# The second block's crossings by token tile, with the norm's gain and shift applied to rows

## The reference

```
for layer in range(DEPTH):                       # second block, DEPTH = 2
    mod = einsum('bd,dn->bn', silu(c), w_ada[layer]) + b_ada[layer]
    sh1, sc1, gt1, sh2, sc2, gt2 = split(mod, 6)
    h = rms_norm(x, g_attn[layer]) * (1.0 + sc1) + sh1
    y = hybrid_mixer(h, ..., w_in[layer], w_out[layer], ...)
    x = x + gt1 * y
    h = rms_norm(x, g_ffn[layer]) * (1.0 + sc2) + sh2
    f = swiglu(h, ...) if layer == 0 else moe_swiglu(h, ...)   # 8 experts, 2 per token
    x = x + gt2 * f
```

## Time and profile before

| | |
|---|---|
| median of 3 runs | 1899.09 us (1898.74 to 1899.36) |
| the profiled execution: its time, its span | 1900.42 us, 1898.6 us |
| PE busy | 1805.7 us, 95% |
| DVE busy | 1424.7 us, 75% |
| ACT busy | 1114.9 us, 59% |
| POOL busy | 392.4 us, 21% |
| the chain that ended last | PE 83%, DVE 6%, issue 6%, ACT 4%, POOL 1% |
| mean granted clock of PE | 0.983 |

### The profile page before, as it was taken

The page is one execution under the profiler, slowest core; times in us unless marked ns, Lnnn a source line. Parts: engine busy times, 40 slices in busy tenths (PEclk is TensorE's granted clock), DMA queues, the critical chain, the costliest instruction groups (busy, mean ns, idle before and its releaser), DMA issues.

```text
span 1898.6 us, 25852 instructions
## 1 busy us (share of the span) xinstructions
PE 1805.7 (95%) x8703; PEld 1469.8 (77%) x8703; DVE 1424.7 (75%) x1667; ACT 1114.9 (59%) x1296; POOL 392.4 (21%) x315
## 2 busy tenths in 40 slices
PE   7899999989999997899989779999999999999997
PEld 6678886858888785788878568888888888888885
DVE  5758874476876585654457659888888888889897
ACT  6745444565443454444355537777777777777775
POOL 3722213463212362200046400000000000000000
PEclk9999999999999999899999989999999999999999
DMA  8348994418897341465544249999999999999994
GB/s 272 112 176 331 338 350 136 154 46 333 335 355 277 90 156 45 158 197 180 191 156 155 98 169 361 384 381 380 380 380 383 378 381 384 381 380 379 382 380 169
DMA packets 237933, 506.37 MB, mean 267 GB/s; under 512 B 23304, under 2 KB 74720, under 8 KB 231712
## 3 DMA queue, kind: packets, MB, share of 16 engines
q1 hardware_dynamic: 225664, 492.85, 71.4%
q0 software_dynamic: 3008, 10.32, 2.0%
q10 hardware_dynamic: 9184, 2.23, 0.5%
HBM read 497.42 MB, written 7.91 MB: 266 GB/s over the span
## 4 chain that ended last, share of the span: by engine, by line
PE 83%; issue 6%; DVE 6%; ACT 4%; POOL 1%; DMA 0%; POOLq 0%; SPq 0%; DVEq 0%; ACTq 0%
PE bank L2391 26%; PE bank L2393 25%; PE bank L2392 25%; PE bank L2510 2%; ACT slab L2080 1%; ACT w_hi L1930 1%; PE bank L2836 1%; DVE slab L1317 1%; PE bank L2602 1%; PE bank L2579 1%; POOL w_lo L848 1%; PE bank L2547 0%; DVE x L1096 0%; PE bank L2561 0%; DMA slab<-in_w_in 0%
## 5 line engine op out<-in xcount | busy, mean ns | idle before, releaser
L999 DVE TENSOR_TENSOR w_lo<-slab,w_hi 128x2048 fp32r<-128x2048 f32 x369 | 848.0, 2309 | 211.6 <-ACT w_hi L1930 211.0
L1930 ACT ACTIVATE w_hi<-slab 128x2048 fp32r<-128x2048 f32 (+2 forms) x421 | 796.7, 1899 | 330.1 <-PE bank L2393 245.7
L2391 PE MATMUL bank<-w_hi,hT_hi 128*128 128x512 f32 (+3 forms) x1664 | 648.5, 390 | 15.1 <-DVE hT_lo L1048 4.3
L2393 PE MATMUL bank<-w_hi,hT_lo 128*128 128x512 f32 (+3 forms) x1664 | 637.3, 383 | 0.0
L2392 PE MATMUL bank<-w_lo,hT_hi 128*128 128x512 f32 (+3 forms) x1664 | 636.8, 383 | 0.0
L2391 PEld LDWEIGHTS bank<-w_hi,hT_hi 128*128 128x128 f32 x1664 | 315.3, 189 | 77.8 <-DVE w_lo L999 8.8
L2393 PEld LDWEIGHTS bank<-w_hi,hT_lo 128*128 128x128 f32 x1664 | 314.7, 189 | 59.4
L2392 PEld LDWEIGHTS bank<-w_lo,hT_hi 128*128 128x128 f32 x1664 | 315.5, 190 | 55.1
L848 POOL TENSOR_TENSOR w_lo<-slab,w_hi 128x512 fp32r<-128x512 f32 (+2 forms) x208 | 256.0, 1266 | 376.6 <-ACT w_hi L1930 359.7
L2391 PE MATMUL bank<-w_hi,hid_hi 128*128 128x512 f32 x680 | 265.7, 391 | 0.7 <-DVE w_lo L999 0.7
L2393 PE MATMUL bank<-w_hi,hid_lo 128*128 128x512 f32 x680 | 265.0, 390 | 0.0
(11 more groups left out here) (254 smaller groups left out, 1229.6 us busy)
## 6 DMA issues: line engine op xcount, KB each, us to landing
slab<-in_w_exp_gate SPq DMA_DIRECT2D x176, 512.0 KB, 7.0
slab<-in_w_exp_up SPq DMA_DIRECT2D x176, 512.0 KB, 7.4
slab<-in_w_exp_down SPq DMA_DIRECT2D x176, 512.0 KB, 6.8
slab<-in_w_ada SPq DMA_DIRECT2D x48, 1024.0 KB, 5.9
slab<-in_w_mlp_in SPq DMA_DIRECT2D x64, 512.0 KB, 6.3
slab<-in_w_mlp_out SPq DMA_DIRECT2D x64, 512.0 KB, 9.0
slab<-in_w_in SPq DMA_DIRECT2D x56, 512.0 KB, 5.1
slab<-in_w_out SPq DMA_DIRECT2D x32, 512.0 KB, 4.7
```

What stands on the lines that cost most here:

```text
L999: dve.tensor_tensor(w_lo[:, q, 0:n], raw(s)[:, 0:n], w_hi[:, q, 0:n].bitcast(F32), ALU.subtract).then_inc(lo_dve, 1)
L1930: act.activation(w_hi[:, q, 0:n], raw(s)[:, 0:n], ACT.Copy).then_inc(hi_done, 1)
L2391: pe.matmul(dst, a_hi, b_hi, start=start, stop=False)
L2393: return pe.matmul(dst, a_lo, b_hi, start=False, stop=stop_)
```

## The change

In the second block each crossing works by token tile. The gain and the shift come as rows that every partition holds: `mod_gains` makes the gain columns early (in the MLP of the layer before), ACT stores them to DRAM with elements of 4 bytes, SP loads gain and shift back, broadcast to 128 partitions (two loads of 512 KB per crossing, `gain_loads`). DVE multiplies each quarter of x by the gain row (`gained_part`, or a whole row in crossing 1) and then scales by the root and adds the shift row in one instruction (`scaled_row`). PE turns the 8 chunks of one token tile, four to a PSUM bank; ACT and DVE write `hT_hi` and `hT_lo` of four chunks at once straight from PSUM. PE finishes the sum of token tile 0 before that of tile 1, and the next products of token tile 0 before those of tile 1. Besides: the output projection's tile 1 moves in front of the last `values()`; the split slots of the MLP's and the experts' tiles start at 3, those of l = 3 at 2; both roots stand behind POOL's weight pieces; the third weight tile of l = 2 and 3 goes from POOL to DVE; the weights of l = 3's first tiles are rounded by ACT before its last `hid_high_part`; and the transposes back to rows in crossing 4 are gone.

```diff
-        BY_DVE1, BY_DVE2 = range(2, 6), range(3, 5)
+        BY_DVE1, BY_DVE2 = range(2, 6), range(2, 5)
...
+            def gain_loads(l, which):
+                m = l - DEPTH
+                sp.wait_ge(gains_out, 32 * (m + 1))
+                if m:
+                    sp.wait_ge(xn_done, TT * (which + 1))
+                for to, src in zip(gain_rows(which), (gains[m, which:which + 1, :].broadcast_to([P, D]), mod_row(m, 3 * which))):
+                    sp.dma_start(to, src).then_inc(gains_in, 16)
...
                     gated(wg, wu, 0)
+                    sp.wait_ge(av_done, UNIT0[l] + UNITS[l])
+                    gain_loads(l, 1)
                     pool_lo(FF0[l] + 1)
...
-                        ff_lo(l, 0, norm_roots)
+                        ff_lo(l, 0)
                         ff_lo(l, 1)
-                    else:
-                        norm_roots()
+                    norm_roots()
...
+            def scaled_row(t, which, root):
+                dve.wait_ge(rstd_done, root)
+                dve.scalar_tensor_tensor(h[:, t, :], h[:, t, :], stat[:, 2, t:t + 1], gain_rows(which)[1], ALU.mult, ALU.add
+                                         ).then_inc(xn_done, 1)
+            def turn(t, b, l, which):
+                o = slice(t * P, (t + 1) * P)
+                dve.wait_ge(hh_done, splits_before(turn_at(l, which)) + 2 * t + b + 1)
+                dve.tensor_tensor(hT_lo[:, 4 * b:4 * b + 4, o], turned_half(l, which, t, b), hT_hi[:, 4 * b:4 * b + 4, o].bitcast(F32),
+                                  ALU.subtract).then_inc(hl_done, 1)
...
+            def cross_gated(l, which):                      # on ACT
+                square_part(0, 0)
+                square_part(1, 0)
+                square_part(0, 1)
+                turn(0, 0, l, which)
+                turn(0, 1, l, which)
+                if not which:
+                    hi_of(l, 2)
+                square_part(1, 1)
+                turn(1, 0, l, which)
+                turn(1, 1, l, which)
...
+            def down_by_token(at):                          # on PE, l = 2's last MLP step
...
+                        part(0, 0, before_last, False)
+                        part(0, 1, before_last, False)
+                        turn_step(J - 1)
+                        part(1, 0, before_last, False)
+                        pe.wait_ge(hidl_done, at + 2 * TT)
+                        last = next_low()
+                        part(0, 0, last, True).then_inc(part_done, 1)
+                        part(0, 1, last, True).then_inc(part_done, 1)
+                        part(1, 1, before_last, False).then_inc(w_used, 1)
+                        part(1, 0, last, True).then_inc(part_done, 1)
+                        part(1, 1, last, True).then_inc(w_used, 1)
+                        turn_row(0, l + 1, 0)
```

More of the change, by code:

```diff
@@ L91 @@
 X_SELW = 7424
-X_HTF = 6144
+X_HTF, X_GAIN = 6144, 2048
 X_ADA, X_ACT, X_ACT2 = 0, 6144, 7168
@@ L160, in stage, with slot @@
     def stage(self, raw=RAW, split=SPLIT, base=0):
[L161 removed]
+        self.last = {self.slot(self.i - 1 - k): self.t - 1 - k for k in range(min(self.split, self.i - self.at))}
         self.i, self.raw, self.split, self.base, self.start, self.at = 0, raw, split, base, self.t, 0
+    def slot(self, i):
+        return (self.base + i % self.split) % SPLIT
     def mark(self):
@@ L1025, in _ @@
-            sums, roots, turned, xns, updates, parted = [0], [0], [0], [0], [0], [0]
-            def turn(gain, shift, banks):
-                m = turned[0]
-                turned[0] += 1
-                def low_of(k):
-                    dve.wait_ge(hh_done, splits_before(m) + k + 1)
-                    dve.tensor_tensor(hT_lo[:, k, :], htf[:, k, :], hT_hi[:, k, :].bitcast(F32), ALU.subtract).then_inc(hl_done, 1)
-                for k in range(KC):
-                    dve.wait_ge(tp_done, KC * m + k - k % 2 + 2)
-                    src = bank[banks[k // 2]][:, (k % 2) * SEQ:(k % 2 + 1) * SEQ]
-                    dve.tensor_scalar(htf[:, k, :], src, gain(k), shift(k), ALU.mult, ALU.add).then_inc(tpe_done, 1)
-                    if k:
-                        low_of(k - 1)
-                low_of(KC - 1)
+                    gained_row(t, 0)
@@ new lines, in norm, with gained_row, gains_loaded @@
+                for t in range(TT):
+                    scaled_row(t, 0, roots[0] - TT + t + 1)
+            sums, roots, turned, gained, updates, parted = [0], [0], [0], [0], [0], [0]
+            def gained_row(t, which):
+                link(dve.tensor_tensor(h[:, t, :], x[:, t, :], gain_rows(which)[0], ALU.mult))
+            def gains_loaded():
+                gained[0] += 1
+                dve.wait_ge(gains_in, 32 * gained[0])
+            def scaled_row(t, which, root):
+                dve.wait_ge(rstd_done, root)
+                dve.scalar_tensor_tensor(h[:, t, :], h[:, t, :], stat[:, 2, t:t + 1], gain_rows(which)[1], ALU.mult, ALU.add
+                                         ).then_inc(xn_done, 1)
@@ L2008, in ada_columns, with gain_stores @@
                         act.dma_start(to.unsqueeze(2), mod_columns(l, v).unsqueeze(2)).then_inc(mods_in[l], 16)
+            def gain_stores(m):
+                act.wait_ge(gains_made, 2 * m + 2)
+                with nc.allow_non_contiguous_dma(reason="columns to rows"):
+                    for which in range(2):
+                        act.dma_start(gains[m, which].rearrange("(k p) -> p k", p=P).unsqueeze(2), modg[:, m, which, :].unsqueeze(2)
+                                      ).then_inc(gains_out, 16)
             def tables():
```

378 lines of the change are left out of this document (238 added, 140 removed).

## The result

The changed kernel takes 1912.57 us (median of 4 runs, 1909.59 to 1915.34) against 1899.09: ratio 1.0070, 95% interval 1.0058 to 1.0083. The prediction was 1894.8, with 1899.5 as the upper end. The profiled execution is the fastest of the four: 1909.59 us, span 1907.8, against a span of 1898.6 before, so it shows 9.2 us of the loss. The mean granted clock is as before, 0.982.

What follows compares the result with a forecast made beforehand. PE was taken as the bound, busy throughout the experts, so earlier gains come through one for one. Crossing terms 1.1 + 2.7 - 1.0 + 1.5 = 4.3 us came off the 1899.09 median: 1894.8, range 1888.5 to 1899.5.

Steps and rivals of the forecast that it cites:

- Hidden work: Gain stores and loads: run inside MLP stages or behind late roots; at crossing 4 a late load costs up to 2 us.
- three signs: Prediction wrong if the root comes before 764, PE waits for a gain load, or crossing 2's clock stays at 1.
- Crossing 1: In front of l = 2's first pass: starts at 635.0 instead of 636.14, 1.1 us gained, bounds 0.8 to 1.2.
- Crossing 2: In front of l = 2's MLP: 2.7 us gained, between 0.7 at half clock and 4.3 at full clock.
- Crossing 3: In front of l = 3: 1.0 us lost, with PE idling 1.8 us for `hid_lo`.
- Crossing 4: In front of the router: products end at 1114.3 against 1115.13, 1.5 us gained, bounds 0.2 and 2.4.
- (c): Crossings 2 and 3: 1.2 GHz level outlasts token tile 0's products, 3.9 us slower, 1903.0 us; chance 0.12.
- (b): Crossings 2 and 3: half clock lasts as before, nothing measurable, 0.3 us gained, 1898.8 us; chance 0.3.
- The sum of the crossings: All four crossings: 1.1 + 2.7 - 1.0 + 1.5 = 4.3 us gained.

Runs made afterwards that it cites:

- runs_loaded_late: Changed kernel with gain stores in runs of 32 bytes and two small gain-vector loads issued in layer 1's attention, not at kernel start: 1897.77 us, ratio 0.9988.
- stores_early: Changed kernel with gain columns made and stored in the same layer's attention instead of its MLP: 1899.32 us, ratio 0.9995.
- root_between: As runs_loaded_late, with row 0's root at the second crossing after six of POOL's eight weight pieces, not behind all: 1899.38 us, ratio 1.0000.
- runs_of_32_bytes: Changed kernel with each gain store writing 128 runs of 32 bytes instead of 1024 4-byte elements, two small loads added at kernel start: 1902.69 us, ratio 1.0014.
- router_row_first: As runs_loaded_late, with DVE splitting row 0's transposes ahead of row 1's sum, scale and gain at the fourth crossing: 1894.87 us, ratio 0.9976.
- before_with_stores: Kernel before plus only the change's four gain stores of 4-byte elements, at the change's places, read by nothing: 1910.11 us, ratio 1.0058.
- before_with_many_runs: Kernel before plus four unread stores at the same places, each of 1024 runs of 32 bytes: 1899.81 us, ratio 1.0004.
- before_with_loads: Kernel before plus four unread loads from DRAM at the same places, each of 1024 4-byte elements: 1898.90 us, ratio 0.9998.

## Why the prediction was wrong

The step that failed is **Hidden work**: "Gain stores and loads for crossings 1 and 3 run in an MLP stage". It costed the stores at nothing because the stage is long and nobody needs them soon. That they land in time is true, PE waits for no gain load. What it left out is what they do to others: l = 1's MLP runs its DMA engines at 400 GB/s with weights that ACT waits for anyway, 6.29 us before the change. In place of 0 the stores cost 9.97 + 2.96 = 12.9 us in the trace after. Alone in the kernel before they cost 10.9; between the change as it is and runs_loaded_late lie 15.6 by the ratios (0.0082 x 1899). The profile, of the fastest execution, does not show the last 3. About 2 of them may be no work of the stores: from the last values to the experts' second pass (the last two rows of the table but the span) this execution took 55.1 us, and the kernels with the same order in crossing 4 (stores_early, root_between, runs_of_32_bytes, runs_loaded_late) took 56.8 to 57.3. The rest is open.

The Trainium skill (DMA: Bandwidth & Descriptors, "Issuing engines are not separate DMA queues") says that DMAs of all issuing engines run on the same 16 DMA engines and interleave. The trace agrees: with two stores of ACT's queue under way, a weight tile of SP's queue came 8 us later.

All three signs by which the prediction was to be known as wrong looked at the crossings, and none of them came: row 0's root came behind all eight pieces, at 775.03 us (767.3 without the 7.75 us that the kernel was late by then), no wait of PE for a gain load is in the trace, and the clock fell in crossing 2. No sign watched the stage in which the change put its new transfers.

The other steps, by the table:

- **Crossing 1**, 1.1 us predicted: 1.3. Right.
- **Crossing 2**, 2.7: 3.1 in the changed kernel, 3.6 and 3.3 in the two repaired ones. From 736.32 to 799.88 the kernel before took 63.6 us, the four kernels that only add transfers to it 62.1 to 64.0, and the changed one 60.4, so the 3.1 is good to about 1 us. POOL held the root as said: eight pieces took 11.81 us, where I put 11.4; PE idled 4.61 (4.5 said). The mean clock over the stage, 0.77 before and 0.93 with the change (the first and the last window below), lies between the two bounds, as assumed. The Trainium skill's rule (SBUF — State Buffer, "SBUF: two separate sides") would have made POOL's eight pieces 12.8 us (an estimate, 10.0 + 4 x 0.7); the trace lies between.
- **Crossing 3**, 1.0 lost: 0.6, 1.0 and 1.1. The wait for `hid_lo` came, 1.40 us (1.8 said).
- **Crossing 4**, 1.5 gained: 0.8 lost, 2.5 lost in runs_loaded_late. From the last sum to the experts' first pass the changed kernel took 25.7 us in place of 27.2, the predicted 1.5 less, but 0.7 was lost in front of it and 1.6 behind it, in the first gate pass, where the mean clock fell from 1.00 to 0.80 (windows below). That pass was left out of the prediction, and I missed that PE, in order, waits 4.25 us for row 0's splits with row 1's transposes behind them. With row 0's splits first the crossing gains 1.0.
- **Rivals.** (c) had the sign by luck, with a wrong mechanism: no low level outlasted token tile 0's products, the granted clock was back at 1.00 from 780 to 785 us. (b), nothing measurable, is near what the repaired change is worth, 2.2 us by the medians.

Crossing 2 and crossing 4 with the gate pass behind it, before, then with the change (there the window of crossing 2 stands last):

```profile
765.70:788.40 22.70, 17.21 (x66) 13.58 (x65) 15.63 (x28) 10.70 (x18) 9.87 (x8) 0.77 0.43 141
1103.30:1130.50 27.20, 18.62 (x105) 13.99 (x104) 19.84 (x50) 8.38 (x19) 2.04 (x3) 0.75 0.44 172
1130.50:1137.30 6.80, 5.79 (x25) 4.49 (x25) 3.06 (x6) 3.22 (x4) 0.00 (x0) 1.00 0.59 189
```

```profile
1112.00:1137.70 25.70, 14.54 (x105) 13.38 (x104) 17.15 (x40) 5.65 (x13) 1.33 (x2) 0.73 0.60 229
1137.70:1146.10 8.40, 7.38 (x25) 5.58 (x25) 3.06 (x6) 3.20 (x4) 0.00 (x0) 0.80 0.48 168
772.40:795.90 23.50, 18.19 (x80) 14.49 (x81) 13.22 (x22) 9.56 (x14) 4.09 (x4) 0.93 0.53 175
```

The sum of the crossings, 4.3, is 4.5 in router_row_first (1.3 + 3.3 - 1.1 + 1.0), and its time, 1894.9, is the one predicted. That is in part luck: it is the change with two repairs, and by its trace it gains 6.4 us, of which 1.8 come in the two attentions, where nothing was predicted; the sum matches largely because the execution profiled before was 1.3 us slower than the median and this one 0.9 faster.

## What to carry to other kernels

Price a transfer also by what it does to those under way: four stores of 4 KB, for which no engine stood waiting, cost more than the crossings that they served brought. Before writing columns of single floats to DRAM, choose a layout in which each partition holds a run of 32 bytes, the length that was free here; if that can't be, put the store where the weight loads rest. And where a kernel reorders work by row, check on each in-order engine what stands behind the first row's wait.

## What the runs showed of the hardware

Stores of 1024 elements of 4 bytes land after 10.6 to 11.9 us even in a quiet stretch (stores_early), and after up to 26.4 in a busy one (before_with_stores). With eight times the bytes, 1024 runs of 32, they land after 3.9 to 14.1 us (before_with_many_runs), and loads of 1024 elements after 3.6 to 14.8 (before_with_loads). In the changed kernel, all four stores:

```profile
DMA to landing us min/median/max: 10.0/13.0/24.3
```

While they are under way all traffic falls from 400 to as low as 76 GB/s, with the DMA engines still shown as busy in the MLP of l = 1 and at 0.37 to 0.49 in that of l = 2. Their whole queue takes 0.7% of the engines' time, as the queue with the harmless ones does. So the share by queue does not show the cause, and the busy share not reliably; the GB/s does. Loads of the same elements, and stores of as many pieces of 32 bytes, cost nothing that could be told, at most 1.3 and 2.5 us by the ends of their intervals.
